# A spare 64 bytes in memory: moving every buffer from h upwards in a one-layer hybrid decoder kernel

## What is computed

```python
mod = (silu(c) @ w_ada + b_ada).reshape(B, 3, 3, 1024)
h = modulate(rms_norm(x, norm_ffn1_g), mod[:, 0, 0], mod[:, 0, 1])
x = x + 0.5 * mod[:, 0, 2] * swiglu(h, ffn1_w_in, ffn1_w_out)   # 1024 -> 2 x 2816 -> 1024
h = modulate(rms_norm(x, norm_mix_g), mod[:, 1, 0], mod[:, 1, 1])
proj = h @ w_mix_in                                             # 1024 -> 1536
ya = causal_multiscale_pool(proj[..., :512], w_pool, pool_scale)
yb = chunked_spatial_gating(proj[..., 512:], gmlp_ln_g, gmlp_ln_b, w_spatial, b_spatial)
x = x + mod[:, 1, 2] * (concatenate([ya, yb]) @ w_mix_out)
h = modulate(rms_norm(x, norm_ffn2_g), mod[:, 2, 0], mod[:, 2, 1])
x = x + 0.5 * mod[:, 2, 2] * swiglu(h, ffn2_w_in, ffn2_w_out)
out = rms_norm(x, norm_final_g)
```

## Time and profile before

| | us |
|---|---|
| median of 3 runs | 876.66 |
| lowest and highest run | 875.43, 879.33 |
| span of the profiled execution | 874.8 |
| TensorE busy in it | 845.0 |
| VectorE busy in it | 641.4 |
| ScalarE busy in it | 379.8 |

### The profile page before, as it was taken

One profiled execution on the slowest core, in us unless ns is written; L12 is line 12 of the kernel. 1 busy time (PEld: TensorE's weight loads), 2 busy tenths in 40 slices (PEclk: granted clock), 3 DMA queues, 4 the chain that ended last, 5 costly groups with the idle time before them and its releaser, 6 DMA issues.

```text
span 874.8 us, 14160 instructions
## 1 busy us (share of the span) xinstructions
PE 845.0 (97%) x5767; PEld 755.0 (86%) x5767; DVE 641.4 (73%) x919; ACT 379.8 (43%) x528; POOL 50.4 (6%) x56
## 2 busy tenths in 40 slices
PE   4899989999999999999999999999999999999996
PEld 3678869888999998888887898899988899999886
DVE  4579977776788877858747779988794588885443
ACT  6233325312466653134424256656511356665323
POOL 0000000000001000000350000000000000100000
PEclk9999998999999999999999999999999999999999
DMA  9997565586566665943534422576663566663222
GB/s 276 291 309 235 160 177 155 167 264 173 133 157 157 160 183 178 299 130 97 154 99 125 143 74 73 140 181 173 193 208 98 137 171 159 155 158 104 86 67 96
DMA packets 214797, 142.02 MB, mean 162 GB/s; under 512 B 6232, under 2 KB 193740, under 8 KB 214732
## 3 DMA queue, kind: packets, MB, share of 16 engines
q1 hardware_dynamic: 209780, 132.19, 52.1%
q0 software_dynamic: 4896, 8.92, 6.2%
q10 hardware_dynamic: 56, 0.01, 0.0%
HBM read 130.08 MB, written 2.10 MB: 151 GB/s over the span
## 4 chain that ended last, share of the span: by engine, by line
PE 81%; DVE 9%; DMA 3%; SPq 2%; issue 2%; ACT 1%; DVEq 0%; ACTq 0%
PE ps L1669 13%; PE ps L1671 13%; PE ps L1670 13%; PE ps L1846 12%; PE ps L1842 12%; PE ps L1844 12%; DVE work L1130 2%; DMA ada_first<-in_w_ada_dram 1%; PE ps L1968 1%; PE ps L1969 1%; PE ps L1970 1%; SPq L469 1%; DVE h_lo L1077 1%; DVE xs L1070 1%; DMA sw_raw<-in_ffn_w_in_dram 1%
## 5 line engine op out<-in xcount | busy, mean ns | idle before, releaser
L1842 PE MATMUL ps<-sums_hi,sw_hi 128*128 128x256 f32 x544 | 152.4, 280 | 4.2 <-ACT ev L832 4.2
L1844 PE MATMUL ps<-sums_lo,sw_hi 128*128 128x256 f32 x544 | 152.9, 281 | 0.0
L1669 PE MATMUL ps<-b_hi,sw_hi 128*128 128x512 f32 (+1 forms) x374 | 143.4, 383 | 0.0
L1670 PE MATMUL ps<-b_lo,sw_hi 128*128 128x512 f32 (+1 forms) x374 | 141.5, 378 | 0.0
L800 ACT CAST sw_hi<-sw_raw 128x1024 fp32r<-128x1024 f32 (+2 forms) x102 | 119.8, 1180 | 31.6 <-DVE sw_raw L1251 19.2
L1842 PE MATMUL ps<-h_hi,sw_hi 128*128 128x256 f32 x408 | 114.3, 280 | 3.0 <-DVE sw_lo_a L1264 3.0
L1846 PE MATMUL ps<-sums_hi,sw_lo_a 128*128 128x256 f32 x408 | 115.7, 284 | 0.0
L1844 PE MATMUL ps<-h_lo,sw_hi 128*128 128x256 f32 x408 | 114.6, 281 | 0.0
L1842 PEld LDWEIGHTS ps<-sums_hi,sw_hi 128*128 128x128 f32 x544 | 102.9, 189 | 4.6 <-issue 4.1
L1264 DVE TENSOR_TENSOR sw_lo_a<-sw_raw,sw_hi 128x1024 fp32r<-128x1024 f32 x68 | 98.9, 1455 | 9.9 <-ACT sw_hi L800 7.6
L1844 PEld LDWEIGHTS ps<-sums_lo,sw_hi 128*128 128x128 f32 x544 | 102.7, 189 | 0.0
(11 more groups left out here) (193 smaller groups left out, 1571.8 us busy)
## 6 DMA issues: line engine op xcount, KB each, us to landing
sw_raw<-in_ffn_w_in_dram SPq DMA_DIRECT2D x170, 256.0 KB, 4.2
sw_raw<-in_w_ada_dram SPq DMA_DIRECT2D x15, 1024.0 KB, 5.6
sw_raw<-in_ffn_w_out_dram SPq DMA_DIRECT2D x32, 384.0 KB, 4.5
sw_raw<-in_ffn_w_out_dram SPq DMA_DIRECT2D x32, 320.0 KB, 3.4
w_raw<-in_ffn_w_in_dram SPq DMA_DIRECT2D x19, 512.0 KB, 5.4
ada_raw<-in_w_ada_dram SPq DMA_DIRECT2D x18, 512.0 KB, 5.4
sw_raw<-sw_raw POOLq DMA_DIRECT2D x34, 256.0 KB, 3.3
ada_first<-in_w_ada_dram SPq DMA_DIRECT2D x14, 512.0 KB, 7.3
```

Source lines behind the costliest of these rows:

```text
L1669: nc.tensor.matmul(dst, w_h, a_h, start=start, stop=False)
L1670: nc.tensor.matmul(dst, w_h, a_l, start=False, stop=False)
L1842: nc.tensor.matmul(dst, w_h[:, k, :], src_hi[:, k, :], start=start and k == 0, stop=False, skip_group_check=True)
L1844: nc.tensor.matmul(dst, w_h[:, k, :], src_lo[:, k, :], start=False, stop=False, skip_group_check=True)
```

## The change

One buffer of 16 float32, 64 bytes of every partition, is declared behind small and ahead of everything from vrow, out_tok and h_hi on. Nothing reads or writes it. All buffers declared after it stand 64 bytes higher; those ahead of it stay where they are. Each engine has the same instructions in the same order, with the same waits.

```diff
@@ -183,6 +183,7 @@
         gs = sb("gs", [P, 3, KD])
         half_gate = sb("half_gate", [P, 2, KD])
         small = sb("small", [P, 64])
+        aside = sb("aside", [P, 16])
 
 
         with ExitStack() as over_h:
```

## The result

The kernel after takes 885.47 us (median of 4 runs, 883.94 to 885.82), the kernel before 877.27 us beside it (4 runs, 875.43 to 879.33). The ratio is 1.0091, 95% interval 1.0072 to 1.011: slower, and above the range of the prediction. The profiled execution of after has a span of 883.6 us, against 874.8.

What follows compares the result with a forecast made beforehand. The prediction took TensorE's pace from matmul to matmul as the bound. Gains of 9.8 us in Strassen units and 4.6 us elsewhere, 14.4 us, turned 876.66 us into 862.3 us, with a range of 858 to 879.

Steps and rivals of the forecast that it cites:

- TensorE's pace sets the time, addresses act through it alone: Whole kernel: TensorE busy 845.0 of 874.8 us, so only its pace or waits matter; the change moves addresses, no instruction.
- the rival without any dependence: Whole kernel: addresses do not matter, time stays at 876.7 us; chance 0.11.
- The positions modulo 128, from which every matmul at 113.3 ns was to follow: Buffers at 0 or 64 modulo 128: the change makes weights and operands equal, so 256-column matmuls follow at 113.3 ns.
- The v projection as evidence: Projection of v: 228 ns with v_split, 233 with w_split, same weights; so equal positions of operand and weights are better.
- Strassen units: Units of 84 matmuls in both FFNs: 9.52 us each, 9.3 us gained in ordinary ones, 9.8 us in all.
- the 53 ns of products 0 to 4: Strassen units: a product with sw_lo_a costs 12 x (117.8 - 113.3) = 53 ns more than products 5 and 6.
- Products of 512 columns and halves: Down, mix-in, mix-out and v products to 226.7 ns, halves of 256 columns from 117.8: sum 4.9 us, taken as 4.6.
- Terms at nothing: Plain products before 125 us (2 us at most), VectorE and ScalarE writes (under 0.4 us), transfers: no gain counted.
- Equal positions are the bad ones for 256 columns: Strassen units: each load at its operand's position costs 13 ns, a unit takes 10.64 us, 901 us in all; chance 0.13.
- Uniform at 117.8 ns: Strassen units: equal positions always give 117.8 ns, 9.895 us a unit, 512 columns still gain, about 876 us; chance 0.12.

Runs made afterwards that it cites:

- e9: Kernel before with spare bytes that put all operands 96 bytes ahead of the weights modulo 256, sw_lo_a with the other weights; 890.62 us, ratio 1.0162.
- e4: Kernel before with 64 spare bytes directly ahead of sw_lo_a, so it moves and the operands stay; 869.93 us, ratio 0.993.
- e2: Kernel before with a spare buffer of 192 bytes instead of after's 64, weights and operands all at 128 modulo 256; 881.93 us, ratio 1.0073.
- e5: Kernel before with 192 spare bytes directly ahead of sw_lo_a, so every load in a unit has its operand at distance 64; 875.64 us, ratio 0.9999.
- e3: Kernel before with 64 spare bytes ahead of the first buffer, so weights and operands all move and keep their distances; 875.01 us, ratio 0.9983.
- e10: Kernel before with everything from h upwards 256 bytes higher, positions modulo 256 unchanged; 876.46 us, ratio 0.9997.
- e11: Kernel before with spare bytes: h and sums 64 ahead of the weights, sw_lo_a at 0 modulo 256, b and y at distance 0; 878.09 us, ratio 1.0021.
- e7: Kernel before with spare bytes: h and sums 64 ahead of all weights, sw_lo_a included, b and y at distance 0; 877.72 us, ratio 1.0009.
- e12: The same kernel as e4 (64 spare bytes ahead of sw_lo_a alone) on another chip with more runs; 870.82 us, ratio 0.9934 to before.
- e1: Kernel before with a spare buffer of 128 bytes instead of after's 64, operands 64 below the high weights; 883.68 us, ratio 1.0089.

## Why the prediction was wrong, step by step

**TensorE's pace sets the time, addresses act through it alone: right.** Instructions, the waits from the first unit on and VectorE's times stayed, the whole 8.8 us lie in the distances between matmul starts, and e9 and e4 are 20.7 us apart by addresses alone. That also rules out the rival without any dependence: with other distances between weights and operands the pace of 256 columns goes from 113.3 to 120.0 ns, by 6%. "TensorE: Matmul & The Clock Gate" of the Trainium skill, Part 2, step 1, says that loading the next weights takes no read bandwidth from the running matmul. It speaks of bandwidth and not of addresses; that addresses couldn't matter was the prediction's inference from it, and this is what the runs contradict. Whether the loads take bandwidth no run here measures.

**The positions modulo 128, from which every matmul at 113.3 ns was to follow: the step that failed.** The prediction reduced every address modulo 128, because buffers start on such multiples there, and no row backed that number. In it before's layout reads as "64 apart" and after's as "equal". Modulo 256 before's is 64 apart and after's 128 apart. The sizes of all buffers were to hand in the kernel; with them the change would have read as a move from 64 to 128, a distance for which no row of before had a pace. There the matmuls of a unit follow at 118.3 and 120.0 ns and not at 113.3.

**The v projection as evidence: the row was read rightly, its reach was not.** The earlier trace rows show distance 0 (v_split) at 228 and -64 (w_split) at 233 ns, and e2 confirms that 0 is best for 512 columns, 226.7. Carried over to 256 columns it fails: there 0 is at the slow end, 120.0 ns. Since those are 34 units of 84 matmuls, even truly equal positions cost time, 0.7% in e2; so this step would have failed by itself. A number of the prediction's own spoke against position as the whole story: it has the plain products at 233 ns, while it takes the mix-in products from 229.4 ns though they stand in the same way. And v_split was at distance 0 in both kernels, so its row could not change.

**Strassen units, forecast -9.8 us, measured +4.9.** The 9.52 us of a unit exists, to the third digit, but with sw_lo_a at -64 and the operands left at 64 (e4), not in the layout of the change. The prediction laid the 53 ns of products 0 to 4 to the change of position from load to load; e4 has such a change and doesn't pay them, and e5, without any, pays them in its trace.

**Products of 512 columns and halves, forecast -4.6 us, measured +3.3 in the down projections and +1.5 in the mixer and FFN 1's half tile.** The value taken, 226.7 ns, is that of distance 0; distance 128 has 232.8.

**Terms at nothing: right.** The start came out 0.8 us shorter, within the 4 us by which the kernels' starts differ anyway; VectorE in a unit is 8.40 us against 8.39, and from the first unit on TensorE waits for no transfer.

**The rivals.** "Equal positions are the bad ones for 256 columns" had the right sign and gave 901 us. Its mechanism exists (e2), but it is not what happened in after, and its price was twice too high: 12 x 13 ns over 1.36 us was to give 1.52 us a product, e2 has 1.44. The price came from products 0 to 4 and laid all their 53 ns to four equal loads; in e2 twelve of them cost 80 ns. "Uniform at 117.8 ns" came nearest in a product, 118.3 to 120.0, but had 512 columns gaining.

**What stays open.** At distance 64 a series runs at one of two paces in the same layout, 113.3 or 117.8 ns for 256 columns and 229.0 or 233.0 for 512: FFN 2's first series takes 9.787 us in e3 and 9.893 in before and e10, y's first half products run at 113 ns in e5's trace and y's later ones at 118, and e4's seven slow units are e11's quick ones. So the distance sets which paces can occur, and something else picks one. The pace was seen to change behind a wait (e7), with a fall of the clock (e12), and from one product to the next where other buffers take over (before); what makes it fall one way or the other no run shows. e5's runs spread over 8 us, which would fit series falling differently from run to run; only one of them was traced, so that is not shown. Nor was it tried to move sw_hi and sw_lo_b apart from each other.

## What to carry to other kernels

Where a kernel loads new weights for each matmul, the distance between the moving operand and the weights, modulo 256 bytes, is worth a measurement: here it spans 2.3% of the time (ratios 0.993 to 1.016) between kernels that have the same instructions. Read the pace from the distance between starts, for each shape apart, since what is best for 512 columns may be worst for 256. And before calling two positions equal, find the modulus by a shift that should change nothing.

## What the runs showed of the hardware

- The pace of float32r matmuls with a load ahead of each depends on the distance between moving operand and weights modulo 256 (e3, e10), at a granted clock of 1.00 in the units read. For 512 columns, loads all at one distance: 226.7 ns at 0, 229.0 at 64 (233.0 in the plain products of before and e7), 232.4 to 233.3 at 32, 96, 128 and -64. For 256 columns: 113.3 or 117.8 at 64 and 113.3 in e1's half tiles at -64, 116.7 or 117.8 at 32, 118.6 to 120.0 at 128, 120.0 at 0 and 96.
- 64 and -64 are not the same at 512 columns: in streams with one distance 229 ns was seen only at 64, and -64 had about 233 in every trace; e1 swapped them in two stages at once.
- With high weights at 64 and every third load at -64, 113.3 ns hold through 24 of the 31 units without waits (e4), while loads all at 64 have 117.8 in all 31 in the traces of e5 and e7. That is not a property of 64 alone: e7's unit 14, all at 64, ran at 113.3.
- A pace is kept for a whole series to the nanosecond: the starts of units 4 to 13 of after and of what follows are all 9980 ns apart. It can change behind a wait of 1.9 us (e7) or with a fall of the granted clock from 1.00 to 0.50 (e12), at unchanged addresses.
